# Thirteen dense products of a two-layer kernel computed by quarters, seven products instead of eight

## The chip, the core and the metric

The kernel runs on one core of a Trainium2 chip. The time is the device time of one execution, in microseconds (us). Three runs of the kernel before gave 1155.68, 1157.85 and 1160.24 us, so its median is 1157.85 us.

TensorE (PE) multiplies into PSUM, VectorE (DVE) and ScalarE (ACT) do elementwise work, GpSimd (POOL) does elementwise work that reads and writes only SBUF, and SyncE (SP) issues the large transfers.

## What is computed

256 tokens of width 1024 in float32 pass through two blocks. Cut to what matters here:

```python
# block 1
proj = rms_norm(x, norm_w) @ w_in
u_s, z_s, q, k, v, z_a, r_s, r_a = split(proj)
y_s = (s5_branch(u_s, ...) * silu(z_s)) @ w_ssm_out        # units so0, so1
y_a = (dilated_attention(q, k, v) * silu(z_a)) @ w_attn_out  # unit ao
m = sigmoid(r_s) * y_s + sigmoid(r_a) * y_a
x = x + m @ w_o                                             # units wo0, wo1
# block 2
proj = rms_norm(x, norm_mix) @ w_in_2    # ..., gate_hg: ghg0, ghg1; gate_da: gda0, gda1
y_hg = (rms_norm(hgrn2(...)) * silu(hog)) @ w_branch_hg     # unit bhg
y_da = rms_norm(diff_attention(...)) @ w_branch_da          # unit bda
mixed = sigmoid(gate_hg) * y_hg + sigmoid(gate_da) * y_da
x = x + mixed @ w_out                                       # units wout0, wout1
x = x + hier_moe(rms_norm(x, norm_moe), router, w1, w3, w2) # 32 experts, 4 at a time
```

## The kernel before

**Units.** Every dense weight is cut on the host into units of 128 x 4096 numbers (2 MB), in the list `FRONT` (line 197). A unit is either 1024 rows by 512 columns (eight blocks of 128 rows), or, for `ao`, `bhg` and `bda`, 512 rows by 1024 columns (four blocks). The units pass through three slots of a ring in SBUF, one after the other. SP loads unit n into slot n % 3 when TensorE has finished unit n - 3 (`load_unit`, line 288); SP's queue keeps the order in which it is written.

**A dense unit on TensorE** is `project` (line 301): for each half of the tokens (128 of 256) and each 512 columns, eight (or four) matmuls of 128 x 128 by 128 x 512 add up in one PSUM bank. Two banks, 0 and 1, take turns (`pj`), two more (`tp`) take transposes. A unit is 16 such matmuls; float32 makes the profile show each matmul as two records, so a unit is 32 records. VectorE or ScalarE reads the bank when it is full and frees it.

**Order of the work.** There is no scheduler: each engine's program is written out by hand and the engines meet at semaphores. After the state-space part and the attention of block 1, TensorE does glu0, glu1, za, then so0, so1, ao; VectorE multiplies each result by its gate (lines 1159, 1167, 1170) into `m_tok`; TensorE transposes it (line 894), ScalarE copies it out as `mT` (line 701), and TensorE does wo0 and wo1, whose results VectorE adds to `xres` (line 1184). Block 2 starts with hf, hq, dq, dk, hi, dv, hog, with the norm and rotation of dq and dk on VectorE (`norm_rope2`, line 1649) between them: TensorE transposes dk only when VectorE has rotated it (`dqk_ready`). Then come eight pieces of differential attention (`da_pieces`), and with each piece one half of a gate unit (ghg0, ghg1, gda0, gda1) so that TensorE has work while VectorE and ScalarE do the softmax. Then bhg, bda (VectorE lines 1765, 1773, 1776), four transposes, wout0, wout1 (line 1781), the router's logits, the choice of experts.

**The experts.** 96 units of 2 MB follow. Ten of them (`AHEAD`) are loaded before the first is used: into the slots of the ring that are free and two other places. SP issues the first of these behind the last load of a dense unit (wout1, which waits for bhg), so none of them starts before about 647 us. From the second use on, a slot is filled again as soon as TensorE has used it (line 342).

**GpSimd** scales and rotates in block 1 (lines 532 to 548) and later only issues small transfers.

## Time and profile before

| | |
|---|---|
| median of three runs | 1157.85 us |
| the profiled execution, its own time | 1155.91 us |
| its span | 1154.0 us |
| TensorE busy | 978.7 us (85%) |
| VectorE busy | 447.0 us (39%) |
| ScalarE busy | 252.0 us (22%) |
| GpSimd busy | 164.8 us (14%) |
| DMA, from 740 us on | about 428 GB/s in nearly every slice |
| granted TensorE clock, mean | 0.941 |

The profile shows one execution. Its span runs from the first to the last instruction, and the execution's own time is 1.9 us longer. Until about 700 us TensorE works nearly without pause and the transfers are light; from about 715 us on the transfers never pause and TensorE works in bursts.

### The profile page before, as it was taken

How to read it: one execution, taken by the hardware profiler on the slowest of the kernel's cores; microseconds unless marked ns; L12 is line 12 of the kernel's file. 1: busy time of each engine (PE TensorE's matmuls, PEld its weight loads, DVE VectorE, ACT ScalarE, POOL GpSimd, SP SyncE). 2: the span in 40 equal slices, each digit the busy share in tenths (PEclk: the TensorE clock that was granted, in tenths of full speed). 3: DMA queues.
4: the chain of work that ended last, by engine and by line, in shares of the span. 5: the costliest groups of instructions: out<-in, count | busy, mean ns of one | idle time of the engine just before them, and what ended most of it. 6: DMA issues, size and time to landing. Idle time of an engine off the chain costs nothing. (4 is left out here: it accounts for less than half of the span.)

```text
span 1154.0 us, 11360 instructions
## 1 busy us (share of the span) xinstructions
PE 978.7 (85%) x4440; PEld 478.6 (41%) x4440; DVE 447.0 (39%) x743; ACT 252.0 (22%) x613; POOL 164.8 (14%) x123
## 2 busy tenths in 40 slices
PE   8999999999989999999899999867585757575755
PEld 7644444446878446644444446312121212121211
DVE  6869999986622123353622413201010101010201
ACT  4464757333421012232122011000000000000000
POOL 1856666661000010000000000000000000000000
PEclk9999999999999999999999998988888988888788
DMA  9333242334224433443132695999999999999996
GB/s 365 154 145 146 74 146 80 139 146 121 74 93 164 166 105 135 154 156 144 57 146 92 272 400 199 430 426 428 430 427 428 427 428 428 430 428 429 428 428 282
DMA packets 22316, 292.84 MB, mean 254 GB/s; under 512 B 2752, under 2 KB 2816, under 8 KB 4480
## 3 DMA queue, kind: packets, MB, share of 16 engines
q1 hardware_dynamic: 21728, 291.69, 62.2%
q0 software_dynamic: 544, 0.56, 0.6%
q8 instruction: 29, 0.48, 0.2%
q14 instruction: 15, 0.12, 0.0%
HBM read 291.18 MB, written 1.05 MB: 253 GB/s over the span
## 5 line engine op out<-in xcount | busy, mean ns | idle before, releaser
L1967 PE MATMUL psum<-mem 128*32 128x512 f32 x1016 | 145.7, 706 | 84.1 <-DMA mem<-in_experts 84.0
L305 PE MATMUL psum<-mem,hT 128*128 128x512 f32 x416 | 183.9, 598 | 1.6 <-ACT xres L645 1.6
L312 PE MATMUL psum<-mem,hT 128*128 128x512 f32 x288 | 126.7, 596 | 2.8 <-ACT xn L645 1.6
L305 PE MATMUL psum<-mem 128*128 128x512 f32 x288 | 125.2, 593 | 2.4 <-ACT mem L1381 1.5
L305 PEld LDWEIGHTS psum<-mem,hT 128*128 128x128 f32 x416 | 78.4, 192 | 95.9 <-issue 95.8
L1986 PE MATMUL psum<-mem 128*32 128x512 f32 x512 | 79.6, 753 | 35.7 <-DMA mem<-in_experts 31.6
L1967 PEld LDWEIGHTS psum<-mem 128*32 128x32 f32 x1016 | 31.1, 119 | 180.3 <-DMA mem<-in_experts 118.5
L312 PEld LDWEIGHTS psum<-mem,hT 128*128 128x128 f32 x288 | 55.7, 196 | 68.3 <-issue 68.3
L305 PEld LDWEIGHTS psum<-mem 128*128 128x128 f32 x288 | 54.2, 190 | 69.0 <-issue 65.1
L319 PE MATMUL psum<-hT,mem 128*128 128x256 f32 x256 | 57.6, 382 | 0.0
L2088 DVE TENSOR_TENSOR mem<-mem,psum 128x512 f32<-128x512 f32 x8 | 5.5, 688 | 129.6 <-PE psum L1967 129.6
L1037 DVE TENSOR_TENSOR_SCAN mem<-small,mem 128x256 f32<-128x256 f32 x64 | 54.3, 909 | 0.0
L1986 PEld LDWEIGHTS psum<-mem 128*32 128x32 f32 x512 | 15.7, 125 | 90.0 <-DMA mem<-in_experts 51.4
L319 PEld LDWEIGHTS psum<-hT,mem 128*128 128x128 f32 x256 | 48.0, 190 | 7.0
L2094 DVE TENSOR_TENSOR xres<-xres,psum 128x512 f32<-128x512 f32 x32 | 22.0, 688 | 72.1 <-PE psum L1998 72.1
L2085 DVE SCALAR_TENSOR_TENSOR mem<-mem,psum 128x512 f32<-128x512 f32 x8 | 5.5, 688 | 89.5 <-ACT mem L1899 89.5
L1998 PE MATMUL psum<-mem 128*128 128x512 f32 x64 | 34.1, 657 | 6.2 <-ACT mem L1903 6.2
L1901 ACT ACTIVATE mem<-psum 128x512 f32<-128x512 f32 x8 | 4.8, 597 | 147.8 <-PE psum L1977 147.8
L1954 PE MATMUL psum<-mem,xn 128*128 128x128 f32 x256 | 30.6, 278 | 7.3 <-DVE xres L2094 6.8
L1897 ACT ACTIVATE mem<-psum 128x256 f32<-128x256 f32 x8 | 3.1, 384 | 146.1 <-PE psum L1973 146.1
L1954 PEld LDWEIGHTS psum<-mem,xn 128*128 128x128 f32 x256 | 29.2, 192 | 13.2 <-issue 11.6
L1903 ACT ACTIVATE mem<-psum 128x512 f32<-128x512 f32 x8 | 4.8, 597 | 128.0 <-PE psum L1986 128.0
(372 smaller groups left out, 1194.0 us busy)
## 6 DMA issues: line engine op xcount, KB each, us to landing
mem<-in_experts SPq DMA_DIRECT2D x95, 2048.0 KB, 35.5
mem<-in_front SPq DMA_DIRECT2D x39, 2048.0 KB, 7.7
mem<-in_front SPq DMA_DIRECT2D x2, 1024.0 KB, 9.9
xn<-in_xT SPq DMA_DIRECT2D x1, 1024.0 KB, 6.3
mem<-in_ssm_b SPq DMA_DIRECT2D x2, 512.0 KB, 11.9
mem<-in_ssm_c SPq DMA_DIRECT2D x2, 512.0 KB, 17.8
xres<-in_x SPq DMA_DIRECT2D x1, 1024.0 KB, 9.6
mem<-in_experts SPq DMA_DIRECT2D x1, 1024.0 KB, 22.2
```

The source lines that it names most:

```text
L305: ins = pe.matmul(dst, lhs[:, k, P * i:P * i + P], w[:, k, c0:c0 + 512], start=(k == 0), stop=(k == nk - 1))
L312: ins = pe.matmul(dst, tokens[:, k, i], w[:, k, :], start=(k == 0), stop=(k == KD - 1))
L319: ins = pe.matmul(dst, w[:, k, P * m:P * m + P], rhs[:, k, :], start=(k == 0), stop=(k == nk - 1))
L1037: ins = dve.tensor_tensor_scan(out=dst[:, b, c], data0=m, data1=src[:, c], initial=0.0, op0=ALU.mult, op1=ALU.add)
L1901: act.activation(hidT_, banks[7], ACT.Copy, scale=0.5).then_inc(hidT_ready, 1)
L1954: ins = pe.matmul(banks[4 + k // 4][:, P * (k % 4):P * (k % 4) + P], xn[:, i, P * k:P * k + P], sel_[:, P * i:P * i + P], start=(i == 0), ...
L1967: ins = pe.matmul(banks[m // 4][32 * q:32 * q + 32, :], xgT[:, k, 32 * q:32 * q + 32], w[q][:, FF * kk:FF * kk + FF], start=(k == 0), stop ...
L1986: ins = pe.matmul(banks[2 + c][32 * q:32 * q + 32, :], hidT[:, k, 32 * q:32 * q + 32], w[q][:, 512 * kk:512 * kk + 512], start=(k == 0), s ...
L1998: pe.matmul(banks[6 + n % 2], selT_[:, P * (n % 2):P * (n % 2) + P], y_[:, 512 * (n // 2):512 * (n // 2) + 512], start=True, stop=True).th ...
L2085: dve.scalar_tensor_tensor(out=act_, in0=th_, scalar=1.0, in1=banks[0], op0=ALU.add, op1=ALU.mult).then_inc(act_ready, 1)
L2088: dve.tensor_tensor(hid_, act_, banks[1], ALU.mult).then_inc(hid_ready, 1)
L2094: dve.tensor_tensor(dst, dst, banks[6 + n % 2], ALU.add).then_inc(added, 1)
```

## The change

Thirteen units (`QUARTERED`: so0, so1, ao, wo0, wo1, ghg0, ghg1, gda0, gda1, bhg, bda, wout0, wout1) are no longer computed by `project`. Activation and weights are split into quarters: tokens in two halves, rows of the weight in two halves, columns in two halves. Seven products of quarters replace eight (Strassen's scheme in Winograd's form):

- s1 = x21 + x22, s2 = s1 - x11, s3 = x11 - x21, s4 = x12 - s2 of the activation, once for each activation, on VectorE (`sums_of`);
- t1 = w12 - w11, t2 = w22 - t1, t3 = w22 - w12, t4 = w21 - t2 of every unit's weights, on GpSimd (`sum_weights`), with 128 x 1024 numbers each;
- P1 = x11 w11, P2 = x12 w21, P3 = s4 w22, P4 = x22 t4, P5 = s1 t1, P6 = s2 t2, P7 = s3 t3 on TensorE (`products`);
- the four quarters of the result from P1 + P2, P1 + P6 + P3 + P5, P1 + P6 + P7 + P5, P1 + P6 + P7 + P4 on VectorE. ScalarE copies P1 and P5 out of PSUM first.

A product of a unit of eight blocks is four matmuls of 128 x 128 by 128 x 256, one of a unit of four blocks is two matmuls by 128 x 512. The products go in the order 1, 5, 6, 2, 3, 7, 4 through three PSUM banks in turn, so the fourth product waits until the first has been taken, and so on across units (`after_taken`); wo0 and wout0 begin with product 4.

The weight sums take 3 x 1024 columns of SBUF, for block 2 those of ring slot 3, so the expert units of slots 3 and 4 are loaded later (slot 3 after wout1, slot 4 after `m2_done`). In the attention pieces the order of VectorE's and TensorE's work changes: the scores use one pair of banks instead of two.

```diff
         def load_unit(sp, n):
             s = n % SLOTS_BLOCKS
             if n >= SLOTS_BLOCKS:
-                pj.to_read(sp, last_fill[FRONT[n - SLOTS_BLOCKS][0]])
+                after_unit(sp, FRONT[n - SLOTS_BLOCKS][0])
...
+        def sums_of(dve, X, x):
+            x11, x12, x21, x22 = halves_of(X)
+            s1, s2, s3, s4 = x_sums[x]
+            link(dve, dve.tensor_tensor(s1, x21, x22, ALU.add), sums_ready)
+            link(dve, dve.tensor_tensor(s2, s1, x11, ALU.subtract), sums_ready)
+            mark(dve.tensor_tensor(s4, x12, s2, ALU.subtract), sums_ready)
+            link(dve, dve.tensor_tensor(s3, x11, x21, ALU.subtract), sums_ready)
+
+        def sum_weights(pool, n):
...
+            pool.wait_ge(slot_loaded[order[name] % SLOTS_BLOCKS], 16 * (order[name] // SLOTS_BLOCKS + 1))
+            if j >= 2:
+                pool.wait_ge(product_full, full(n - 2, 4))
+            pool.tensor_tensor(t1, w12, w11, ALU.subtract).then_inc(weights_ready, 1)
+            pool.wait_ge(weights_ready, sums_done(n, 1))
+            if j >= 1:
+                pool.wait_ge(product_full, full(n - 1, 6))
+            pool.tensor_tensor(t2, w22, t1, ALU.subtract).then_inc(weights_ready, 1)
+            pool.wait_ge(weights_ready, sums_done(n, 2))
+            if j >= 1:
+                pool.wait_ge(product_full, full(n - 1, 5))
+            pool.tensor_tensor(t4, w21, t2, ALU.subtract).then_inc(weights_ready, 1)
+            pool.tensor_tensor(t3, w22, w12, ALU.subtract).then_inc(weights_ready, 1)
+
+        def multiply(pe, n, p, lhs, rhs):
+            nk = lhs.shape[1]
+            for k in range(nk):
+                ins = pe.matmul(product_bank(n, p), lhs[:, k, :], rhs[:, k, :], start=(k == 0), stop=(k == nk - 1))
+            ins.then_inc(product_full, 1)
...
+        def take_p6(dve, n):
...
+            dve.tensor_tensor(p16, p1, product_bank(n, 6), ALU.add).then_inc(taken, 1)
+        def put_11(dve, n, dst):
...
+            dve.tensor_tensor(dst, taken_of(n)[0], product_bank(n, 2), ALU.add).then_inc(taken, 1)
+        def put_12(dve, n, dst):
...
+            dve.tensor_tensor(dst, taken_of(n)[2], product_bank(n, 3), ALU.add).then_inc(taken, 1)
+        def add_p5(dve, n, dst):
...
+            return dve.tensor_tensor(dst, dst, taken_of(n)[1], ALU.add)
+        def take_p7(dve, n):
...
+            dve.tensor_tensor(p167, p16, product_bank(n, 7), ALU.add).then_inc(taken, 1)
+        def sum_22(dve, n, dst):
...
+            return dve.tensor_tensor(dst, taken_of(n)[1], taken_of(n)[3], ALU.add)
+        def put_21(dve, n, dst):
...
+            dve.tensor_tensor(dst, taken_of(n)[3], product_bank(n, 4), ALU.add).then_inc(taken, 1)
...
+        def use_quarters(dve, n, use, then=None):
+            take_p6(dve, n)
+            use_11(dve, n, use, then)
+            use_12(dve, n, use, then)
+            take_p7(dve, n)
+            use_22(dve, n, use, then)
+            use_21(dve, n, use, then)
...
             pe.wait_ge(glu_used, 8)
-            project_all(["so0", "so1"], PJ_SO, gs)
+            for j in range(2, 4):
+                pj.after_read(pe, PJ_ZA + j)
+            ORDER, TURNED = ORDERS["so0"], ORDERS["wo0"]
+            for n in range(2):
+                products(pe, n, gs, X_GS, ORDER)
             pe.wait_ge(oa_ready, 4)
...
+            products(pe, nth["ao"], oaT, X_OA, ORDER)
...
@@ the second block, SyncE
-            sp.wait_ge(m_done, 4)
-            load_ahead(sp, 3)
...
+            tp.to_read(sp, TP_HG + 1)
+            load_ahead(sp, 6)
+            load_ahead(sp, 7)
+            da.to_read(sp, 7)
+            load_ahead(sp, 5)
...
+            load_ahead(sp, 3)
@@ the second block, VectorE
             norm_rope2(1)
+            dve.wait_ge(hT2_ready, 1)
+            sums_of(dve, hT, X_H2)
```

In `use_11` and its three neighbours VectorE then multiplies the finished quarter by its gate; for wo0, wo1, wout0 and wout1 (`add_to_x`) it adds the parts to `xres`, eleven operations a unit.

GpSimd, behind the last of its scaling work of block 1. Before, its program goes from seven small transfers to five more and ends:

```order
L554 DMA small<-in_da_out_norm 128x128
L554 DMA small<-in_da_lambda 128x256
L1336 DMA small<-in_norm_moe 128x8x1 [waits lam_in]
L1336 DMA small<-in_w_router_group 128x8x4
L1336 DMA small<-in_w_router_expert 128x8x32
```

Now the sums of five units stand between them (L543 is t1, L547 t2, L551 t4, L552 t3); of these, so0, so1 and the start of ao:

```order
L838 DMA small<-in_da_lambda 128x256
L543 TENSOR_TENSOR mem<-mem 128x1024 [waits slot2_loaded,s_full]
L547 TENSOR_TENSOR mem<-mem 128x1024 [waits weights_ready]
L551 TENSOR_TENSOR mem<-mem 128x1024 [waits weights_ready]
L552 TENSOR_TENSOR mem<-mem 128x4x256
L543 TENSOR_TENSOR mem<-mem 128x1024 [waits slot0_loaded]
L547 TENSOR_TENSOR mem<-mem 128x1024 [waits product_full,weights_ready]
L551 TENSOR_TENSOR mem<-mem 128x1024 [waits product_full,weights_ready]
L552 TENSOR_TENSOR mem<-mem 128x4x256
L543 TENSOR_TENSOR mem<-mem 128x1024 [waits product_full,slot1_loaded]
```

Four operations of 128 x 1024 a unit are added, 52 in all, all with both inputs and the output in SBUF.

VectorE, the results of so0, so1 and the start of ao. Before (`th_s` is the gate, pj0 and pj1 the two banks):

```order
L1159 SCALAR_TENSOR_TENSOR mem<-mem,psum 128x512 [waits th_s_ready,pj0_full]
L1159 SCALAR_TENSOR_TENSOR mem<-mem,psum 128x512 [waits th_s_ready,pj1_full]
L1159 SCALAR_TENSOR_TENSOR mem<-mem,psum 128x512 [waits th_s_ready,pj0_full]
L1159 SCALAR_TENSOR_TENSOR mem<-mem,psum 128x512 [waits th_s_ready,pj1_full]
L1167 SCALAR_TENSOR_TENSOR mem<-mem,psum 128x512 [waits pj0_free,th_a_ready,pj0_full]
```

Now, so0 alone (L615 takes P6, L621 P7, L626 adds P2, L632 P3, L647 P4; L637 and L642 add P5; L1442 is the gate):

```order
L615 TENSOR_TENSOR mem<-mem,psum 128x256 [waits p1_copied,product_full,th_s_ready,sums_ready]
L626 TENSOR_TENSOR mem<-mem,psum 128x256 [waits taken,product_full]
L1442 SCALAR_TENSOR_TENSOR mem<-mem 128x256 [waits taken]
L632 TENSOR_TENSOR mem<-mem,psum 128x256 [waits taken,product_full,q_step]
L637 TENSOR_TENSOR mem<-mem 128x256 [waits taken,p5_copied]
L1442 SCALAR_TENSOR_TENSOR mem<-mem 128x256 [waits q_step]
L621 TENSOR_TENSOR mem<-mem,psum 128x256 [waits taken,product_full,q_step]
L642 TENSOR_TENSOR mem<-mem 128x256 [waits taken,p5_copied]
L1442 SCALAR_TENSOR_TENSOR mem<-mem 128x256 [waits q_step]
L647 TENSOR_TENSOR mem<-mem,psum 128x256 [waits taken,product_full]
L1442 SCALAR_TENSOR_TENSOR mem<-mem 128x256 [waits taken]
```

Two operations of 128 x 512 a unit, each with one input in PSUM, have become eleven of 128 x 256: five with an input in PSUM and six with both inputs in SBUF.

TensorE, the end of so0 and the start of so1. Before (the second half of the tokens of so0, then so1):

```order
L305 MATMUL psum<-mem 128x512 [waits pj1_free]
L305 MATMUL psum<-mem 128x512 x7
L305 MATMUL psum<-mem 128x512 [waits pj0_free,slot0_loaded]
L305 MATMUL psum<-mem 128x512 x7
L305 MATMUL psum<-mem 128x512 [waits pj1_free]
```

Now (P3, P7 and P4 of so0, then P1, P5 and P6 of so1):

```order
L557 MATMUL psum<-mem 128x256 [waits sums_ready,p5_copied]
L557 MATMUL psum<-mem 128x256 x3
L557 MATMUL psum<-mem 128x256 [waits sums_ready,weights_ready,taken]
L557 MATMUL psum<-mem 128x256 x3
L557 MATMUL psum<-mem 128x256 [waits weights_ready,taken]
L557 MATMUL psum<-mem 128x256 x3
L557 MATMUL psum<-mem 128x256 [waits taken,slot0_loaded]
L557 MATMUL psum<-mem 128x256 x3
L557 MATMUL psum<-mem 128x256 [waits sums_ready,weights_ready,taken]
L557 MATMUL psum<-mem 128x256 x3
L557 MATMUL psum<-mem 128x256 [waits sums_ready,weights_ready,taken]
L557 MATMUL psum<-mem 128x256 x3
```

Sixteen matmuls of 512 columns a unit have become 28 of 256, and every group of four waits for VectorE (`taken`) or ScalarE (`p1_copied`, `p5_copied`) to have taken the group three before it.

## Rows read from the trace of the kernel before

**Rows 1.** The page: busy time by engine, and GB/s in 40 slices.
```profile
PE 978.7 (85%) x4440; PEld 478.6 (41%) x4440; DVE 447.0 (39%) x743; ACT 252.0 (22%) x613; POOL 164.8 (14%) x123
...
GB/s 365 154 145 146 74 146 80 139 146 121 74 93 164 166 105 135 154 156 144 57 146 92 272 400 199 430 426 428 430 427 428 427 428 428 430 428 429 428 428 282
```

**Rows 2.** TensorE in order, 325 to 420 us: start, length, line, records, wait.
```profile
356.70 13.98 PE L319 MATMUL psum<-hT,mem 128*128 128x256 f32 x64
370.52 41.36 PE L305 MATMUL psum<-mem 128*128 128x512 f32 x96
413.39 1.09 PE L894 MATMUL psum<-con,mem 128*128 128x128 f32 x8 [1.51 <-DVE mem L1170]
```

**Rows 3.** TensorE in order of time, 408 to 575 us.
```profile
416.67 20.84 PE L305 MATMUL psum<-mem 128*128 128x512 f32 x48 [0.73 <-ACT mem L701]
...
438.22 7.03 PE L305 MATMUL psum<-mem 128*128 128x512 f32 x16
...
530.63 1.04 PE L1444 MATMUL psum<-con,mem 128*128 128x128 f32 x8
...
559.48 7.13 PE L305 MATMUL psum<-mem,hT 128*128 128x512 f32 x16
570.28 0.33 PE L1541 MATMUL psum<-con,mem 128*128 128x128 f32 x1 [3.66 <-DVE mem L1736]
```

**Rows 4.** TensorE in order of time, 560 to 715 us.
```profile
582.78 7.03 PE L305 MATMUL psum<-mem,hT 128*128 128x512 f32 x16
...
599.53 7.03 PE L305 MATMUL psum<-mem,hT 128*128 128x512 f32 x16
...
633.04 7.03 PE L305 MATMUL psum<-mem 128*128 128x512 f32 x16
...
649.01 13.97 PE L305 MATMUL psum<-mem 128*128 128x512 f32 x32 [0.78 <-ACT mem L1381]
...
667.72 20.84 PE L305 MATMUL psum<-mem 128*128 128x512 f32 x48 [0.74 <-ACT mem L1381]
```

**Rows 5.** The chain that ended last, from 700 us: start, length, what.
```profile
714.66 7.07 PE psum L1967 x64
...
736.68 29.91 DMA mem<-in_experts
```

**Rows 6.** Vector engine by shape, 320 to 715 us: busy, mean ns, wait.
```profile
L1146 DVE TENSOR_TENSOR mem<-mem 128x256 f32<-128x256 f32 x8 | 3.4, 425 | 0.3
...
L1776 DVE TENSOR_TENSOR mem<-mem 128x512 f32<-128x512 f32 x4 | 2.8, 692 | 0.1
...
L1705 DVE TENSOR_TENSOR mem<-mem,small 128x1024 f32<-128x1024 f32 x2 | 2.4, 1224 | 0.1
```

**Rows 7.** GpSimd by shape, the whole span.
```profile
L533 POOL TENSOR_TENSOR mem<-mem 128x1024 f32<-128x1024 f32 x2 | 4.4, 2217 | 0.0
```

**Rows 8.** GpSimd in order of time, 159 to 176 us.
```profile
162.40 1.26 POOL L547 TENSOR_TENSOR mem<-mem 128x512 f32<-128x512 f32 x1
163.74 1.59 POOL L548 TENSOR_TENSOR mem<-mem 128x512 f32<-128x512 f32 x1
```

**Rows 9.** Vector engine in order of time, 159 to 176 us.
```profile
161.22 0.69 DVE L1026 TENSOR_TENSOR mem<-mem,psum 128x512 f32<-128x512 f32 x1
...
162.54 1.67 DVE L1028 TENSOR_TENSOR mem<-mem 128x512 f32<-128x512 f32 x1
```

**Rows 10.** Vector engine in order of time, 500 to 575 us.
```profile
523.75 0.42 DVE L1662 TENSOR_TENSOR xn<-mem,con 128x256 f32<-128x256 f32 x1
...
528.81 0.42 DVE L1667 TENSOR_TENSOR mem<-xn 128x256 f32<-128x256 f32 x1
539.27 0.69 DVE L1679 SCALAR_TENSOR_TENSOR mem<-mem,psum 128x512 f32<-128x512 f32 x1 [10.04 <-ACT mem L1393]
```

**Rows 11.** SyncE, 515 to 540 us: start of the first, length, count.
```profile
516.21 14.94 SPq L293 DMA_DIRECT2D mem<-in_front  x2
```

**Rows 12.** Transfers of line 293, 480 to 600 us: issue to landing.
```profile
DMA to landing us min/median/max: 7.4/7.7/8.1
```

More of the change, by code:

```diff
@@ L427, in build @@
                         + [(f"glu{n}", PJ_GLU + 4 * n + 3) for n in range(2)]
-                        + [(f"so{n}", PJ_SO + 2 * n + 1) for n in range(2)]
-                        + [("za", PJ_ZA + 3)]
-                        + [("ao", PJ_AO + 3)] + [(f"wo{n}", PJ_WO + 2 * n + 1) for n in range(2)]):
+                        + [("za", PJ_ZA + 3)]):
             last_fill[name] = s
+        QUARTERED = ("so0", "so1", "ao", "wo0", "wo1", "ghg0", "ghg1", "gda0", "gda1", "bhg", "bda", "wout0", "wout1")
@@ new lines, in build, with product_bank @@
+        FIRST_BANK = {"so0": 0, "so1": 7, "ao": 0, "wo0": 14, "wo1": 20, "ghg0": 0, "ghg1": 7, "gda0": 14, "gda1": 21,
+                      "bhg": 0, "bda": 7, "wout0": 0, "wout1": 0}
+        def product_bank(n, p):
+            name = QUARTERED[n]
+            width = 2048 // blocks_of(n)
+            if ORDERS[name][0] == p == 4:
+                return banks[0][:, 0:width]
+            at = ORDERS[name].index(p) - (1 if ORDERS[name][0] == 4 else 0)
+            three = (0, 1, 6) if name in GATES else (4, 5, 6) if name in ("ao", "bhg", "bda") else (6, 7, 5) if name == "wout1" else (1, 2, 3)
+            return banks[three[(FIRST_BANK[name] + at) % 3]][:, 0:width]
@@ new lines, in taken_of @@
+        def taken_of(n):
+            name, width = QUARTERED[n], 2048 // blocks_of(n)
+            part = lambda ap: [whole[:, 0:width] for whole in four(ap)]
+            if n < OF_FIRST:
+                return part(area[:, 16896:18944]) + [area[:, 13824:14336] if name == "ao" else area[:, 18688:18944]]
+            if name in GATES:
+                return part(xn[:, 1, :]) + [None]
+            return part(work[:, 2048:4096] if n < nth["wout0"] else area[:, 12288:13312]) + [xn[:, 1, 0:512]]
@@ new lines, in use_12, with use_22 @@
+        def use_12(dve, n, use, then=None):
+            c12 = taken_of(n)[4]
+            put_12(dve, n, c12)
+            link(dve, add_p5(dve, n, c12), q_step)
+            link(dve, use(0, 1, c12), q_step)
+            if then:
+                then(0, 1)
+        def use_22(dve, n, use, then=None):
+            p5 = taken_of(n)[1]
+            link(dve, sum_22(dve, n, p5), q_step)
+            use(1, 1, p5).then_inc(taken, 1)
+            dve.wait_ge(taken, used(n, C22))
+            if then:
+                then(1, 1)
@@ L1590, in _ @@
-            pe.wait_ge(m2_done, 4)
-            turn(TP_M2, 4, by_k(m2))
-            for s in range(2):
-                tp.after_read(pe, TP_M2 + 2 + s)
+            products(pe, nth["bda"], daT, X_DA, ORDER)
+            turn_quarters(pe, TP_M2, m2, m2_done)
+            for s in range(TP_M2, TP_M2 + 2):
+                tp.after_read(pe, s)
+            n0, n1 = nth["wout0"], nth["wout1"]
+            products(pe, n0, m2T, X_M2, TURNED[0:1])
+            for s in range(TP_M2 + 2, TP_M2 + 4):
+                tp.after_read(pe, s)
@@ new lines, in _, with of_hg @@
+                if a == 3:
+                    for s in range(2):
+                        tp.after_read(dve, TP_HG + s)
+                    sums_of(dve, hgT, X_HG)
+            put_21(dve, nth["gda1"], gate(3)[:, 1, 0:256])
+            da_out(*pieces[7][0:3])
+            da.after_read(dve, 7)
+            norm_sums(oda_, ods_ready)
+            def of_hg(i, half, src):
+                c = slice(512 * half, 512 * half + 512)
+                return dve.scalar_tensor_tensor(out=m2[:, i, c], in0=th_hg[:, i, c], scalar=1.0, in1=src, op0=ALU.add, op1=ALU.mult)
@@ new lines, in of_da, with both @@
+            def of_da(i, half, src):
+                c = slice(512 * half, 512 * half + 512)
+                return dve.scalar_tensor_tensor(out=th_da[:, i, c], in0=th_da[:, i, c], scalar=1.0, in1=src, op0=ALU.add, op1=ALU.mult)
+            def both(i, half):
+                c = slice(512 * half, 512 * half + 512)
+                dve.tensor_tensor(m2[:, i, c], m2[:, i, c], th_da[:, i, c], ALU.add).then_inc(m2_done, 1)
+            n = nth["bhg"]
+            take_p6(dve, n)
+            norm_out(oda_, odr_ready, ogain).then_inc(oda_ready, 1)
@@ new lines, in _ @@
+            dve.wait_ge(gates_ready, 2)
+            use_11(dve, n, of_hg)
+            use_12(dve, n, of_hg)
+            take_p7(dve, n)
+            use_22(dve, n, of_hg)
+            for s in range(2):
+                tp.after_read(dve, TP_DO + s)
+            sums_of(dve, daT, X_DA)
+            use_21(dve, n, of_hg)
+            dve.wait_ge(gates_ready, 4)
+            use_quarters(dve, nth["bda"], of_da, both)
+            for s in range(TP_M2, TP_M2 + 4):
+                tp.after_read(dve, s)
```

497 lines of the change are left out of this document (334 added, 163 removed).

## The prediction

> **What bounds the kernel now.** I read the page first. TensorE is busy 978.7 of 1154 us, and from the slice at 721 us on the transfers run at 428 GB/s without a gap [rows 1]. So there are two stages with different limits. The chain that ended last shows the border: the first use of an expert unit stands at 714.66 us, and from 736.68 us on the chain is made of transfers [rows 5]. After the first two units are used, 86 units are still to come, each 2.10 MB at 428 GB/s = 4.9 us, 421 us in all. Nothing in the change touches them. They start when TensorE frees the first slots, so **the end moves by as much as the first use of an expert unit moves**, if the ten units loaded ahead are there by then. They are: six now go out behind each other from the end of bhg on and are done about 20 us later, slot 4 follows `m2_done`, and behind wout1 come the slots 1 or 2 and 3 and half a unit, 2.5 x 4.9 = 12 us, while TensorE needs the first expert unit 18 us after wout1 (667.72 + 28.4 = 696.1 us to 714.66 us).
>
> Before the border TensorE is the limit [rows 2 to 4], with short waits for VectorE and ScalarE where one unit feeds the next (1.51 us at 413.39 us, 3.66 us at 570.28 us). VectorE and GpSimd are half idle there. The question is therefore what thirteen units cost TensorE, and what now waits for VectorE.
>
> **What TensorE saves.** A record of 512 columns costs 41.36 / 96 = 0.431 us, one of 256 columns 13.98 / 64 = 0.218 us [rows 2], weight load hidden in both. A unit was 32 x 0.431 = 13.8 us. It becomes 56 x 0.217 = 12.1 us (or 28 x 0.431 = 12.1), so 1.7 us less, 13 times: 22 us. A product of quarters is 1.73 us.
>
> **What VectorE and GpSimd get.** VectorE without a neighbour needs 0.42 us for 128x256, 0.69 for 128x512, 1.22 for 128x1024 with both inputs in SBUF [rows 6], and 0.69 for 128x512 with one in PSUM [rows 9]. Eleven operations a unit are 4.7 us, or 7.6 us for a unit of four blocks, below the 12.1 us of TensorE. GpSimd's four sums cost four times 2.2 us [rows 7] = 8.8 us, also below. If they ran side by side, little would be lost.
>
> They don't run side by side. At 162.54 us VectorE issues an addition with both inputs in SBUF. GpSimd has been at work on an SBUF operation since 162.40 and ends at 163.66; the addition ends at 164.21, 1.67 us instead of 0.69: it has waited for the whole of GpSimd's operation. GpSimd's next one, due at 163.74, takes 1.59 instead of 1.26 [rows 8, 9]. The addition at 161.22, with one input in PSUM, takes its 0.69 us beside a busy GpSimd [rows 9]. So additions with both inputs in SBUF and GpSimd's sums take turns, and a queued sum gets in between two such additions that wait for one another by a semaphore. GpSimd's operations were 1.3 us there; the new sums are 2.2 us.
>
> The Trainium skill, page "SBUF — State Buffer", section "Who interferes with whom", gives the rule: a VectorE instruction with two SBUF inputs and a GpSimd instruction that reads SBUF exclude each other for the whole instruction, one with a single SBUF input does not take part. By it the gate multiplications from SBUF (SCALAR_TENSOR_TENSOR) are blocked too, which no row here shows; with them free the sum below would be about 12 us less.
>
> Of VectorE's eleven operations a unit, six have both inputs in SBUF. When are GpSimd's sums due? t2 waits for P6 of the unit before, t4 and t3 follow at once, t1 of the next unit waits for P4. So in each unit they run from its 5.5th us to past its end, exactly when VectorE takes the results. I work each stretch out from its start, in us, with 0.3 us from the last matmul to VectorE's start.
>
> *so0, so1, ao* (before 370.52 to 416.67, 46.2 us). First a new wait: banks 1 to 3 are shared with za, whose last result goes through ScalarE and VectorE, 1.2 us. Then, with so0 at 0: t2(so1) 5.5 to 7.7; first gate operation to 8.1; t4 to 10.3; add P5 to 10.7; t3 to 12.9; gate to 13.4; take P7 to 13.9; t1(ao), due at 12.4, to 15.6; sum_22 16.0, gate 16.5, P4 taken 17.0. so1 has begun at 12.1, its P6 needs the bank of so0's P4 and is due at 15.6: it waits to 17.1. So so1 ends at 25.7 instead of 24.2, ao likewise at 39.2. Behind ao the same chain is 15 operations of 0.72 us (with the sums of the two branches) and four sums: from P6 at 32.6, the last addition ends at 50.1. Transposes of one half, then wo0 at 50.8. With 1.2 in front: 52.0, **+5.8**. Without taking turns it would end at 43.3, -2.9.
>
> *wo0, wo1* (416.67 to 445.1, 28.4). Two units and a transpose 25.2; only wo1's t2, t4, t3 stand against `add_to_x`; wo1's first two products wait 2.3 us. **-0.9**; without turns -3.4.
>
> *dk.* GpSimd may start on ghg0's four sums when ghg0 lands: issued at 516.21 [rows 11], 7.7 us on its way [rows 12], 524 us. There VectorE rotates dk, from 523.75 twelve linked operations of 128x256, both inputs in SBUF, until 529.2 [rows 10], and TensorE transposes it at 530.63, 1.4 us later [rows 3]. Four sums of 2.1 to 2.2 us get in between: 8.4 us, so dk is ready at 537.6 and TensorE waits **7.0**. Nothing later is idle to take it back. This one hits nothing that the change speaks of, it is only in the way.
>
> `sums_of(hT)` (four of 0.69) stands in VectorE's gap of 10 us before 539.27 us [rows 10] and costs nothing; if dk comes late it still has 14 us of hog beside it.
>
> *Gates* (559.48 to 633.04, 73.6 us: 23.3, then three pairs of 16.75 [rows 3, 4]). The first combine now goes before the norm, so the 3.66 us wait goes. But the mask of piece 1 comes behind three operations of 1.22 us and t2, t4 of ghg1, at 14.5 us, and since one pair of banks serves the scores, TensorE's scores(2) wait for it from 9.9 us; exponent, combine and P2 follow: the pair takes 23.2 us. Each later pair is 12.1 + 2.5 for scores, values, transposes = 14.6, plus 2.4 because P4 waits for P2 to be taken behind a combine with three SBUF operations that wait for t2 and t3: 17.0. Sum 74.2, **+0.6**; without turns 18.8 + 3 x 14.6 = 62.6, -11.0.
>
> *bhg, bda* (633.04 to 667.72, 34.7). bhg with its transposes 15.7. bda's P5 needs the bank of P7 and s1 of daT, which VectorE reaches behind norm (two of 1.22 between t2, t4, t3), four gate operations and t1(wout0): 22.3 instead of 18.1. bda ends at 33.1, and as behind ao the last addition is 10.5 us later; wout0 at 44.3. **+9.6**; without turns -0.9.
>
> *wout0, wout1* as wo0, wo1: **-0.9**; without turns -3.4.
>
> Sum with strict turns: 5.8 - 0.9 + 7.0 + 0.6 + 9.6 - 0.9 = +21.2 us. I take 2 us off, because unlinked additions can pass in one gap of GpSimd: +19. The profiled execution was 1155.9 us (span 1154.0, and 1.9 around it), 1.9 below the median of 1157.85: 1155.9 + 19 = **1175 us**.
>
> **Rivals.**
> - *The sums are cheap.* VectorE and GpSimd hardly meet, because VectorE's queue runs ahead or the scaling's pattern (broadcast inputs) was what made GpSimd hold it. Then -2.9 - 3.4 + 0 - 11.0 - 0.9 - 3.4 = -21.6, 1134 us. For it: VectorE's idle share of 61% [rows 1]. Against it: rows 8 and 9, and the semaphore behind nearly each addition.
> - *Half of it.* Turns are taken, but the gate multiplications go free, or stalls in one unit push the sums of the next out of the way. Then dk and the norms still pay, the tails pay half: about 0, 1148 to 1164 us, here 1156.
> - *GpSimd becomes the bound.* Its 1024-wide operation takes 2.6 us instead of 2.2 (half in the way, strided quarters); about 22 of its 52 sums stand on the chain, 22 x 0.4 = 9 us more, and four a unit with VectorE's turns come to 13 us, above the 12.1 of TensorE: it decides from there on. 1155.9 + 21 + 9 = 1186 and up to 1195 us. The slower side in the extreme.
> - *The 256-column matmuls don't cost half,* the weight load shows. [Rows 2] speak against it, 0.218 to 0.431; I give it nothing of its own.
>
> **Chances.** Forecast 0.52 (1164 to 1188), cheap sums 0.20 (1130 to 1148), half 0.18, GpSimd the bound 0.10. The range: 1143 to 1190 leaves most of the cheap case below and half of the last above. A measurement tells 0.5%, 5.8 us, from no change. Faster than 1152: 0.20 + a third of the half case = 0.26. Within: 0.11. Slower than 1163.6: 0.52 + 0.10 and the rest, 0.63.
>
> **What would show it.** In the trace after: dense units of 56 records at 0.218 us. VectorE's two-SBUF-input additions of 128x256 with a mean of 1 us or more, those from PSUM at 0.42 to 0.48. TensorE idle about 7 us before the transpose of dk, 10 us before wo0 and before wout0, 1.5 us inside so1 and ao. First use of an expert unit at about 733 us, and from there the same 430 us to the end. Wrong would be: two-input additions at 0.42 us (then cheap sums), or a first expert use that moves without the end moving.

## The result and the profile after

The changed kernel takes 1190.72 us (median of 4 runs, 1187.65 to 1199.75) against 1157.08 us of the kernel before in the same session (1155.68 to 1160.24). The ratio is 1.0285, with a 95% interval of 1.0242 to 1.0328: **slower by 2.9%, some 33 us**. Forecast were 1175 us and a range up to 1190: the right side, some 16 us too little of it, and just outside the range.

The profiled execution took 1187.65 us (span 1185.9), the lowest of its four times. The page of the changed kernel (compare [rows 1]; PEclk is the granted TensorE clock in tenths, slice by slice):

```profile
PE 972.4 (82%) x4668; PEld 528.5 (45%) x4668; DVE 580.1 (49%) x874; ACT 262.9 (22%) x635; POOL 294.8 (25%) x175
...
PEclk9999999999999979998999878998888888878788
...
GB/s 368 145 133 142 81 133 141 93 158 87 117 91 150 175 107 124 161 142 71 72 142 83 273 248 217 375 429 426 429 426 429 427 429 429 429 427 429 428 429 286
```

TensorE should have lost 22 us of busy time and lost 6. VectorE is busy 133 us longer and GpSimd 130. VectorE has 131 operations more; the kernel without the weight sums (below) has the same 874 and is busy 504.6 us with them, 58 us longer than before. The other 75 of the 133 us is time in which an operation counts as running and waits. The stream of the experts' weights at 428 GB/s begins one slice later than before.

TensorE in order of time (start, length, line, records, the wait before them), to be read against [rows 2 to 4]:

```profile
416.00 1.09 PE L1581 MATMUL psum<-con,mem 128*128 128x128 f32 x4 [5.43 <-DVE mem L1453]
418.76 1.11 PE L1581 MATMUL psum<-con,mem 128*128 128x128 f32 x4 [1.67 <-DVE mem L1453]
...
422.47 13.38 PE L557 MATMUL psum<-mem 128*128 128x256 f32 x56
...
438.90 8.58 PE L557 MATMUL psum<-mem 128*128 128x256 f32 x32 [3.05 <-DVE xres L692]
...
545.41 1.97 PE L1759 MATMUL psum<-con,mem 128*128 128x128 f32 x8 [6.59 <-DVE mem L1986]
547.17 15.83 PE L311 MATMUL psum<-mem,hT 128*128 128x512 f32 x32
...
577.12 1.97 PE L557 MATMUL psum<-mem,hT 128*128 128x256 f32 x8 [0.41 <-issue]
...
631.02 1.99 PE L557 MATMUL psum<-mem,hT 128*128 128x256 f32 x8 [2.28 <-DVE mem L626]
...
672.25 13.06 PE L557 MATMUL psum<-mem 128*128 128x512 f32 x24 [3.90 <-DVE mem L530]
690.74 1.09 PE L1581 MATMUL psum<-con,mem 128*128 128x128 f32 x4 [5.43 <-DVE mem L2110]
...
714.46 3.35 PE L557 MATMUL psum<-mem 128*128 128x256 f32 x8 [3.05 <-DVE xres L692]
...
746.71 0.62 PE L2318 MATMUL psum<-hT,mem 128*32 128x512 f32 x2
```

Every new wait of more than 1.6 us has VectorE as its releaser: behind ao (5.43 and 1.67), within the wo pair (3.05), before the dk transposes (6.59), in the later pairs of gates (2.28 to 2.88), in bhg (1.77), in bda (3.90), behind bda (5.43 and 1.67), within the wout pair (3.05). None has GpSimd. The last row is the first use of an expert: 746.71 us in place of 714.66 [rows 5], so **32.05 us later**. From there to the end of the span it is 439.2 us, before 439.3. The border between the stages held.

What VectorE and GpSimd did before the dk transposes, in the changed kernel, GpSimd first:

```profile
531.98 2.43 POOL L543 TENSOR_TENSOR mem<-mem 128x1024 f32<-128x1024 f32 x1 [90.13 <-DMA mem<-in_front]
534.49 2.40 POOL L547 TENSOR_TENSOR mem<-mem 128x1024 f32<-128x1024 f32 x1
536.98 2.41 POOL L551 TENSOR_TENSOR mem<-mem 128x1024 f32<-128x1024 f32 x1
539.34 2.52 POOL L552 TENSOR_TENSOR mem<-mem 128x1024 f32<-128x1024 f32 x1
```

```profile
531.77 0.43 DVE L1981 TENSOR_TENSOR xn<-mem,con 128x256 f32<-128x256 f32 x1
532.23 2.46 DVE L1982 TENSOR_TENSOR xn<-mem,con 128x256 f32<-128x256 f32 x1
534.72 2.45 DVE L1983 TENSOR_TENSOR xn<-mem,con 128x256 f32<-128x256 f32 x1
537.21 2.45 DVE L1984 TENSOR_TENSOR xn<-mem,con 128x256 f32<-128x256 f32 x1
539.70 2.44 DVE L1985 TENSOR_TENSOR mem<-xn 128x256 f32<-128x256 f32 x1
542.18 0.42 DVE L1986 TENSOR_TENSOR mem<-xn 128x256 f32<-128x256 f32 x1
```

Four operations of VectorE take 2.45 us, the ones before and behind them 0.42 to 0.43. Each ends some 0.3 us behind the end of a GpSimd sum. Four sums, four operations held up, one each: turns. Both engines show as busy all the while.

### The profile page after: what moved, and what is told of

Read it like the earlier page. It is cut to its first block and busy times, and to the rows that moved or that the text cites. A ratio compares the mean times of both kernels' runs of the same rounds, so it can differ in the third digit from the quotient of the medians.

```text
span 1185.9 us, 12251 instructions
## 1 busy us (share of the span) xinstructions
PE 972.4 (82%) x4668; PEld 528.5 (45%) x4668; DVE 580.1 (49%) x874; ACT 262.9 (22%) x635; POOL 294.8 (25%) x175
## 5 line engine op out<-in xcount | busy, mean ns | idle before, releaser
L557 PE MATMUL psum<-mem 128*128 128x256 f32 (+1 forms) x452 | 128.8, 442 | 15.2 <-DVE xres L692 6.1
L311 PE MATMUL psum<-mem,hT 128*128 128x512 f32 x288 | 128.0, 602 | 1.6 <-ACT xres L931 1.6
L318 PE MATMUL psum<-mem,hT 128*128 128x512 f32 x288 | 126.7, 596 | 2.9 <-ACT xn L931 1.6
L557 PEld LDWEIGHTS psum<-mem 128*128 128x128 f32 x452 | 89.3, 202 | 48.5 <-issue 29.5
L318 PEld LDWEIGHTS psum<-mem,hT 128*128 128x128 f32 x288 | 55.7, 196 | 68.3 <-issue 68.3
L311 PEld LDWEIGHTS psum<-mem,hT 128*128 128x128 f32 x288 | 54.8, 193 | 69.2 <-issue 69.0
L543 POOL TENSOR_TENSOR mem<-mem 128x1024 f32<-128x1024 f32 x13 | 32.2, 2476 | 196.6 <-DMA mem<-in_front 180.7
L547 POOL TENSOR_TENSOR mem<-mem 128x1024 f32<-128x1024 f32 x13 | 31.5, 2424 | 114.7 <-PE psum L557 114.5
L2441 DVE COPY mem<-psum 128x512 f32<-128x512 f32 x8 | 5.5, 691 | 70.6 <-PE psum L2337 70.6
L827 POOL TENSOR_TENSOR mem<-mem 128x512 f32<-128x512 f32 x16 | 21.7, 1354 | 72.5 <-DVE mem L1317 52.2
L2349 PE MATMUL psum<-mem 128*128 128x512 f32 x64 | 33.4, 645 | 6.2 <-ACT mem L2254 6.2
L2252 ACT ACTIVATE mem<-psum 128x512 f32<-128x512 f32 x8 | 4.8, 597 | 148.0 <-PE psum L2328 148.0
```

The costliest lines, as they stand in the source:

```text
L311: ins = pe.matmul(dst, lhs[:, k, P * i:P * i + P], w[:, k, c0:c0 + 512], start=(k == 0), stop=(k == nk - 1))
L318: ins = pe.matmul(dst, tokens[:, k, i], w[:, k, :], start=(k == 0), stop=(k == KD - 1))
L543: pool.tensor_tensor(t1, w12, w11, ALU.subtract).then_inc(weights_ready, 1)
L547: pool.tensor_tensor(t2, w22, t1, ALU.subtract).then_inc(weights_ready, 1)
L557: ins = pe.matmul(product_bank(n, p), lhs[:, k, :], rhs[:, k, :], start=(k == 0), stop=(k == nk - 1))
L827: link(pool, pool.tensor_tensor(Hr[:, b], cos_t[:, b], scan_re[:, b], ALU.mult), pool1)
```

## The experiments

My theory at this point was that of the prediction: an operation of VectorE with both inputs in SBUF and a GpSimd sum exclude each other and take turns, and VectorE's chains, late for that, stop TensorE. New was a second part: the granted clock. From 650 to 697 us, core 0, the changed kernel and then the kernel before (PE, PEld, DVE, ACT, POOL busy, then PEclk, DMA share, GB/s):

```profile
650.00:697.00 47.00, 32.68 (x87) 15.62 (x86) 36.83 (x37) 7.41 (x13) 24.21 (x9) 0.83 0.68 273
```

```profile
650.00:697.00 47.00, 44.51 (x128) 21.07 (x126) 8.25 (x12) 5.54 (x13) 0.00 (x0) 1.00 0.87 372
```

Before, the clock stood at 1.00, all of it at 2.4 GHz; now it is 0.83, part of the stretch at 1.2 GHz. The rival theories were that VectorE's added operations alone are too many, that GpSimd's sums come late by themselves, or that TensorE is slow behind the waits for another reason than its clock.

Three of the kernels below (without the sums, with copies, with memsets) leave the weight sums out and compute other numbers; they serve for their times alone.

**Without the sums.** The body of `sum_weights` is left out, and TensorE multiplies plain quarters:

```
-            t1, t2, t3, t4 = weight_sums_of(n)
+            t1, t2, t3, t4 = w12, w22, w12, w21
-                    pe.wait_ge(weights_ready, sums_done(n, ...))
```

> Left out: the 52 weight sums on GpSimd; TensorE multiplies plain quarters in their place, so the numbers differ and the count of instructions on TensorE and VectorE does not. Theory (the loss is made by VectorE taking turns with GpSimd's sums, and the rest of it by the clock that falls after the waits so made): first use of an expert, 746.7 us in the changed kernel, falls to 680 to 690, since the units then cost what my no-turns terms say (-2.9, -3.4, 0, -11.0, -0.9, -3.4, sum -21.6 from 714.7, so 693; less what the clock no longer loses), and the whole run is 1130 to 1140 us, faster than before. Rival A (VectorE's own added operations, not the turns, make the loss): first use of an expert stays above 725 and the run above 1168. Rival B (GpSimd's sums are late by themselves and TensorE waits for them, not for VectorE): also near 1135, but VectorE's operations on two SBUF inputs would keep their length in the tail of ao (2.71 us each); the theory wants them at 1.2.

Measured: 1131.76 us, ratio to before 0.9773 (0.9739 to 0.9808). The first expert is used at 690.48 us. My sum without turns was 1134. VectorE's operations behind ao were back at the lengths of before (my text said 1.2 us for these 512 columns; alone they take 0.69):

```profile
404.35 0.69 DVE L1429 SCALAR_TENSOR_TENSOR mem<-mem 128x512 f32<-128x512 f32 x1
405.08 0.69 DVE L1433 SCALAR_TENSOR_TENSOR mem<-mem 128x512 f32<-128x512 f32 x1
```

So the seven products and VectorE's work are worth 26 us, and the 52 sums cost 59. The rival of VectorE's added operations falls: they are all still here. The rival of the late sums had these operations stay at 2.71 us, and in the trace of the changed kernel no wait of TensorE between ao and the first expert has GpSimd as its releaser.

**What of a GpSimd operation holds VectorE up.** All four subtractions are replaced by a copy of one quarter, or by a memset, of the same shape:

```
-            pool.tensor_tensor(t1, w12, w11, ALU.subtract).then_inc(weights_ready, 1)
+            pool.tensor_copy(t1, w12).then_inc(weights_ready, 1)      # one kernel
+            pool.memset(t1, 0.0).then_inc(weights_ready, 1)           # the other
```

> GpSimd copies one quarter where it subtracted two (one input from SBUF in place of two), so the numbers differ. Theory (two reading inputs are needed on GpSimd's side too): as without the sums, VectorE's operations at 1.2 us, first use of an expert at 685 to 695. Rival (one input is enough): VectorE's operations in the tail of ao wait for the copy's length, 1.2 us plus what the copy takes, and first use of an expert stays above 700.

> GpSimd writes zeros where the weight sums stood (a memset of the same shape, nothing read), so the numbers differ. Asks what of GpSimd's work makes VectorE take turns. Theory (it is reading two operands from SBUF): VectorE's two-input operations in the tail of ao take 1.2 us again in place of 2.71, first use of an expert at 685 to 695. Rival (any GpSimd operation holds the SBUF port): they still wait for the memset's length, and first use of an expert lies above 700.

Measured: copy 1137.35 us (0.9818), first expert at 696.62; memset 1129.57 us (0.9750), first expert at 688.45. With the copies, GpSimd and then VectorE:

```profile
405.49 1.04 POOL L552 COPY mem<-mem 128x1024 f32<-128x1024 f32 x1
```

```profile
405.75 1.32 DVE L1449 SCALAR_TENSOR_TENSOR mem<-mem 128x512 f32<-128x512 f32 x1
407.11 0.69 DVE L1453 SCALAR_TENSOR_TENSOR mem<-mem 128x512 f32<-128x512 f32 x1
```

With the memsets:

```profile
406.94 0.95 POOL L543 MEMSET mem<- 128x1024 f32 x1 [4.01 <-PE psum L557]
```

```profile
407.39 0.69 DVE L642 TENSOR_TENSOR mem<-mem 128x512 f32<-128x512 f32 x1
```

The multiplication that came 0.26 us behind a copy's start took 1.32 us: it waited until about the copy's end. The addition inside a memset's time took its 0.69. So one operand read from SBUF is enough, and writing alone does nothing. VectorE's busy time over the whole run says the same of all the operations: 580.1 us in the changed kernel, 520.1 with copies, 504.8 with memsets, 504.6 without sums. For the copy this is the rival's mechanism; its bound of 700 us was mine and wrong, because a copy takes 1.04 us where a sum takes 2.35, and VectorE waited 15.5 us for copies in all and 75.5 for sums. The Trainium skill, "SBUF — State Buffer", section "Who interferes with whom", says the same: a VectorE instruction with two SBUF inputs contends with a GpSimd instruction that reads SBUF, and not with one that only writes it. By that rule the gate multiplications take part too, and the trace agrees: L1453 took 2.71 us in the changed kernel and 0.69 without the sums. That page of the Trainium skill frees a VectorE instruction with a single SBUF input only outside the 2-port perf modes, a condition that the prediction left out and that no run here tests.

**The first gate unit's sums by themselves.** First, one line in the changed kernel, ahead of the sums of the second block:

```
             pool.wait_ge(m_done, 4)
+            pool.wait_ge(dqk_ready.sem, 2)
             for n in range(OF_FIRST, len(QUARTERED)):
```

> One line more: GpSimd begins the four weight sums of the first gate unit only once the operands of the dk transposes are there. Theory: TensorE's 6.59 us wait before the dk transposes goes, and with it the 2.8 us that the following 36 records took longer at the lower clock: 9.6 us together, 1181 us (ratio to before 1.0205). The sums then run beside dk's 64 products of TensorE, 16.7 us, and are done before the first gate product. Rival A (the wait only moves: the first gate unit then waits for its sums): 0 to 3 us, 1188 to 1190, with a wait of 5 us or more before the first product with a weight sum. Rival B (clock does not answer to the wait): 6.6 us, 1184, with the 32 records after it still at 15.8 us.

Measured: 1180.91 us, 9.8 less than the changed kernel's 1190.72, ratio to before 1.0190 (1.0155 to 1.0225). The wait before the dk transposes is gone, the records behind it take 13.90 us, and there is no wait before the first gate product:

```profile
542.25 1.04 PE L1760 MATMUL psum<-con,mem 128*128 128x128 f32 x8
543.12 13.90 PE L311 MATMUL psum<-mem,hT 128*128 128x512 f32 x32
```

Then the reverse: the kernel before, with these four sums alone (two waits of SyncE for them, before transfers into the places that they use, are left out here):

```
+            pool.wait_ge(slot_loaded[n % SLOTS_BLOCKS], 16 * (n // SLOTS_BLOCKS + 1))
+            for c, (x, y) in enumerate(((w12, w11), (w22, t[0]), (w21, t[1]), (w22, w12))):
+                pool.tensor_tensor(t[c], x, y, ALU.subtract).then_inc(spare_sums, 1)
```

> The kernel before, with only the four GpSimd sums of the first gate unit's weights added (results unused), in the place where the changed kernel has them. Theory: they alone make the wait before the dk transposes, 6.6 us, and 2.8 us through the clock behind it: 9 to 10 us over the kernel before, 1167 us. Rival A (the wait needs the whole change, for instance the later landing of transfers or VectorE's backlog): under 2 us, 1157 to 1159. Rival B (the turns cost but TensorE keeps its clock): 6.6 us, 1164.

Measured: 1166.41 us, ratio 1.0077 (1.0049 to 1.0106), 8.7 us; in its trace the first expert is used at 724.51 us, 9.85 later.

```profile
537.56 1.97 PE L1457 MATMUL psum<-con,mem 128*128 128x128 f32 x8 [6.68 <-DVE mem L1680]
539.32 15.88 PE L306 MATMUL psum<-mem,hT 128*128 128x512 f32 x32
```

Taken out or put in, four sums that no product needs for over 30 us make the same wait and the same slow 40 records. The two waits of SyncE cost nothing: from the first matmul of bhg to the first expert it is 81.65 us, in the kernel before 81.62. The kernel that has them alone is measurably slower than the kernel before.

**The clock's own part.** The waits stay, but TensorE works through them, on an unused bank: first at dk alone, then also in the two waits behind ao and behind bda and in those within the wo and the wout pair.

```
             project_all(["dv"], PJ_DV, hT)
+            for _ in range(14):
+                pe.matmul(banks[7][:, 0:256], ident, con[:, 0:256], start=True, stop=True)
             pe.wait_ge(dqk_ready.sem, 2)
```

> Fourteen matmuls of 256 columns into an unused bank ahead of the wait before the dk transposes, about 6 us of TensorE, so that it works where it waited 6.59 us. The wait for VectorE itself stays. Theory (the clock falls after the wait): the 32 records behind take 13.9 us again in place of 15.8 and the transposes 1.0 in place of 2.0; time 1188 us, 2.8 less. Rival (the records behind are slow for another cause, GpSimd's sums or the DMA in SBUF): no change in them, 1190.5.

> The changed kernel with matmuls into an unused bank wherever TensorE waited over 3 us on the path: 11 and 3 ahead of the two waits in each tail (ao, bda), 6 ahead of wo1 and of wout1, 14 ahead of the dk transposes. The waits for VectorE stay. Measures what the clock alone took. Theory (a lower clock behind each wait is a cost of its own): dk 2.9 us as with its matmuls alone, the wo pair 1.2 + 1.5, the wout pair 2.0 + 1.5 + 0.3: 9 us, 1181 to 1183. Rival (only the wait before dk mattered, the others are slow for the port or the transfers): 1187 to 1188.

Measured: 1187.76 us (ratio 1.0251, 1.0216 to 1.0285) and 1181.89 us (1.0206, 1.0172 to 1.0240). The first of these intervals overlaps that of the changed kernel, so its 3.0 us rest on the rows:

```profile
542.13 6.21 PE L1803 MATMUL psum<-con 128*128 128x256 f32 x28
548.91 1.09 PE L1759 MATMUL psum<-con,mem 128*128 128x128 f32 x8 [0.57 <-DVE mem L1988]
549.84 13.90 PE L311 MATMUL psum<-mem,hT 128*128 128x512 f32 x32
```

VectorE is as late as ever, but the transposes take 1.09 us in place of 1.97 and the 32 records 13.90 in place of 15.83. With all these places filled, the stretch from the transposes behind ao (415.88 us there) to the first expert (738.91) is 323.0 us, in the changed kernel 330.7 (416.00 to 746.71): the filling gave back 7.7 us. It is not all that the clock took, because the wait of 3.90 us in bda stayed empty. The 24 records behind that one took 13.06 us in the changed kernel at a mean granted clock of 0.80, and 10.73 at 1.00 in the kernel without sums.

**Smaller sums.** If the turns go one for one, the size of GpSimd's operation is what VectorE pays at each. So every sum was made in 2 and in 4 operations on parts of its columns:

```
+            def in_pieces(dst, a, b):
+                cols = dst.shape[2] // 2                                    # 4, 8
+                for c in range(2):
+                    part = slice(cols * c, cols * c + cols)
+                    ins = pool.tensor_tensor(dst[:, :, part], a[:, :, part], b[:, :, part], ALU.subtract)
+                ins.then_inc(weights_ready, 1)
-            pool.tensor_tensor(t1, w12, w11, ALU.subtract).then_inc(weights_ready, 1)
+            in_pieces(t1, w12, w11)
```

> Each of the 52 weight sums on GpSimd is made in two operations of half the columns. If GpSimd's 2.45 us for 1024 columns has a small fixed part, a half takes 1.25 to 1.3 us. Theory (one operation of VectorE, one of GpSimd, in turn): the wait of each VectorE operation for its turn halves, so dk's wait of 6.59 us stays near 6.6 (the same GpSimd time, 9.8 us, is alternated with more VectorE operations, each of which lets one half through), while the chains in the tails, where VectorE's operations are fewer than GpSimd's, lose 1.2 us each less: three in the tail of ao, three unlinked additions twice, some five in the tails of bhg and bda: 10 to 14 us, 1177 to 1181. Rival A (VectorE is locked out as long as GpSimd has work, whatever its pieces): no change, 1190. Rival B (the overhead of 52 more operations and the later sums decide): above 1193, with waits of TensorE for GpSimd.

> As before, in four operations of a quarter of the columns each, 0.65 us by the same rule. Theory: the waits of the tails go down again by half of what they were, 3 to 5 us less than with halves (1173 to 1178), until GpSimd, which now lets a VectorE operation in every 0.65 us, delivers its sums late to TensorE. Rival A: 1190. Rival B: above 1193 and above the time with halves.

Measured: halves 1169.25 us (1.0098, 1.0070 to 1.0125), quarters 1154.85 us (0.9966, 0.9949 to 0.9983). That is 21 and 36 us less than the changed kernel, about twice what I had expected. VectorE behind ao, in the changed kernel, with halves, and with quarters:

```profile
406.91 2.71 DVE L1453 SCALAR_TENSOR_TENSOR mem<-mem 128x512 f32<-128x512 f32 x1
...
412.42 2.71 DVE L1449 SCALAR_TENSOR_TENSOR mem<-mem 128x512 f32<-128x512 f32 x1
```

```profile
411.13 1.63 DVE L1460 SCALAR_TENSOR_TENSOR mem<-mem 128x512 f32<-128x512 f32 x1
```

```profile
409.38 1.10 DVE L1460 SCALAR_TENSOR_TENSOR mem<-mem 128x512 f32<-128x512 f32 x1
```

Less the 0.69 of the operation itself: 2.02, 0.94, 0.41 us of waiting, half of it at each halving. "Locked out as long as GpSimd has work" is refuted. The wait before the dk transposes follows the same count: 6.07 us with halves, whose eight pieces all find a turn among the chain's twelve operations, and 3.00 with quarters, whose sixteen don't. I had the tails in mind and left the gates out. From the first matmul of the gates to the first of bhg it was 73.0 us in the changed kernel, 69.9 with halves and 62.7 with quarters, so with quarters the gates gained 10 of the 36 us.

**Together.** Quarters and eighths, both with the line that delays the first gate unit's sums:

> Weight sums in quarters, and the sums of the first gate unit begun only behind the operands of the dk transposes. With quarters alone that wait was 3.0 us, with 14.81 and 1.90 us in place of 13.9 and 1.04 behind it. Theory: 4.8 us less than with quarters alone, 1150, faster than before by 0.7%. Rival: the moved sums press on a later place and the time stays at 1155.

> The same with eighths (128 columns for each partition). A GpSimd operation took 2.8, 1.44, 0.87 us as it was halved twice while VectorE took its turns; VectorE's 512-column operations 2.71, 1.64, 1.10 against 0.69 without sums. The part of GpSimd's that holds VectorE up is 2.02, 0.95, 0.41, so an eighth should hold it for 0.2 us and VectorE's operation take 0.9. Theory: the tails get 3 us shorter again, if GpSimd keeps up: 1144 to 1148. Rival: with a turn at each of its 8 pieces and 0.69 us given away at each, a sum takes 7 us, four of them 28, and TensorE waits for sums in ao and the gates: 1155 to 1170.

Measured: quarters 1147.05 us (0.9913, 0.9885 to 0.9940), eighths 1146.09 us (0.9897, 0.9869 to 0.9925). The two are not to be told apart. The moved sums gained more than the 4.8 us that I expected over quarters alone. With eighths a new wait stands before wout0, the first with GpSimd as the releaser, and slow records behind it:

```profile
658.54 6.62 PE L564 MATMUL psum<-mem 128*128 128x256 f32 x16 [2.07 <-POOL mem L540]
```

A sum's four or eight pieces each give a turn away: the 52 sums took 131 us of GpSimd's time whole, 147 in halves, 173 in quarters, 206 in eighths. So the last kernel mixes them: quarters for wo0 and wout0, eighths for the rest, the delayed sums of the first gate unit, and 3 and 6 matmuls into an unused bank (`fill`) in the two waits behind ao and behind bda:

```
+            m = 4 if QUARTERED[n] in ("wo0", "wout0") else 8
             ...
                 for i in range(2):
+                    if half:
+                        fill(pe, (3, 6)[i])
                     pe.wait_ge(done, (2, 3) [i] if half else (3, 4)[i])
```

> A version made of what the runs show: weight sums in eighths, but in quarters for wo0 and wout0 (with eighths the first product of wout0 waited 2.07 us for its sums), the first gate unit's sums begun behind the operands of the dk transposes, and 3 and 6 matmuls into an unused bank ahead of the two waits in each tail. Theory: against eighths everywhere (1146) it regains the 2.07 us before wout0, some 3 us of clock behind it (the first 16 records took 6.62 us in place of 3.62) and 1 to 2 us behind the tail of ao: 1139 to 1142, 1.3% faster than before. Rival (what is regained there comes back as a later landing of the experts' weights or as a wait for sums in another unit): 1145 to 1147.

Measured: 1142.48 us (1141.43 to 1145.91) against 1160.84 of the kernel before in that session, ratio 0.9850 (0.9827 to 0.9872): **1.5% faster than the kernel before, 4% faster than the changed kernel**. The first expert is used at 703.05 us. What each of the changes in it gave is not measured apart. The wait for GpSimd is gone, and the 16 records take 4.76 us (3.62 at the full clock):

```profile
659.31 4.76 PE L566 MATMUL psum<-mem 128*128 128x256 f32 x16
```

Where the time lies, from the traces, in us. The borders are the first transposes behind ao, the first matmul of the first gate unit, the first transposes behind bda, the first use of an expert:

| | to ao's end | gates' start | bda's end | experts | end |
|---|---|---|---|---|---|
| before | 413.4 | 146.1 | 105.0 | 50.2 | 439.3 |
| changed | 416.0 | 161.1 | 113.6 | 56.0 | 439.2 |
| halves | 412.9 | 157.0 | 106.9 | 51.3 | 439.5 |
| quarters | 410.6 | 152.9 | 97.6 | 53.3 | 439.5 |
| mixed | 413.5 | 147.8 | 90.1 | 51.7 | 439.2 |
| no sums | 408.8 | 146.2 | 86.0 | 49.5 | 439.4 |

The last column never moves: all of it is won and lost before the experts. The gates and the branches behind them hold the most, 28 us between the changed kernel and the one without sums.

## Why the prediction was nearly right, and where it failed

The mechanism was right: turns of one operation each, gate multiplications included, idle time before the dk transposes that nothing takes back, an end that moves with the first expert. **The step that failed is the sum of the turns' price: it holds a wait of TensorE at its own length and the records behind it at full speed.** In the runs they were slower at a lower granted clock. My terms with and without turns are 42.8 us apart (+21.2 and -21.6); the first expert of the changed kernel and of the one without sums are 56.2 us apart. Apart from the gates, every stretch from wo0 on came out dearer than forecast. By stretch, forecast and measured (start of each stretch, after against before, in us):

- so0, so1, ao, up to wo0 (422.47 against 416.67): +5.8 and **+5.8**. In part luck: without the sums it was -1.7 where I had -2.9, and the turns added 7.5 where I had 8.7.
- wo0, wo1 (446.52 to 454.32 behind them): -0.9 and **+2.0**. Two things were missing: the three unlinked additions of `add_to_x` did not pass in one gap of GpSimd but took a turn each (L692 from SBUF has a mean of 932 ns over 24, from PSUM 417), so the wait was 3.05 us and not 2.3; and the records ran slow: 13.38 us for 56 in place of 56 x 0.218 = 12.2, and 8.58 for 32 in place of the 7.14 that they took with the wait filled.
- dk: +7.0 and **+9.6**. The wait was 6.59, close to the forecast; 0.93 + 1.93 us come from the clock behind it.
- gates (577.12 to 650.14): +0.6 and **-0.5**. This is luck: two errors met. Without the sums the gates took 59.6 us (forecast 62.6), and the turns added 13.4 (forecast 11.6).
- bhg, bda, up to wout0 (697.13): +9.6 and **+12.3**. The wait for `sums_of` in bda, 3.90 us, stands behind the norm, whose two operations took 1.94 and 2.24 us on average, and a sum took 3.2 to 3.3 us where it had to let such an operation of 1024 columns through.
- wout0, wout1 to the first expert: -0.9 and **+2.6**. The clock is the larger part of the difference: the first 16 records took 5.64 us in place of 3.62, and the eight behind the wait 3.35 in place of the 1.97 that they took with the wait filled.

Their sum is 32 us; mine was 21.2. TensorE's own time up to the first expert shows where the 11 us between them lie. The changed kernel, the kernel before and the one without sums (PE, PEld, DVE, ACT, POOL busy, PEclk, DMA share, GB/s):

```profile
0.00:746.71 746.71, 677.64 (x2796) 439.06 (x2796) 525.42 (x787) 246.36 (x603) 294.80 (x175) 0.97 0.40 148
```

```profile
0.00:714.66 714.66, 684.48 (x2569) 388.60 (x2569) 392.29 (x656) 235.50 (x581) 164.79 (x123) 0.99 0.42 156
```

```profile
0.00:690.48 690.48, 664.38 (x2797) 433.04 (x2797) 449.87 (x787) 246.13 (x603) 164.85 (x123) 0.99 0.43 160
```

TensorE's idle time rose from 30.2 to 69.1 us, by 38.9, where my sum has about 43 (21.2, and the 22 of work saved). So the waits were not underpriced as a whole. Its busy time fell by 6.8 where I had 22, and with the same records but without the sums it falls by 20.1. The absent term is in the records: they are 13.3 us longer in the changed kernel than in the one without sums. That the clock makes all of it is not shown, but its mean is 0.97 there against 0.99, and filling the waits gave back 7.7 us.

GpSimd's operation was mis-sized too: "2.2 us" in my sum, 2.35 alone and 2.42 to 2.58 on average in its four places. How much of the end that moved is not measured. And the step "I take 2 us off, because unlinked additions can pass in one gap of GpSimd" is refuted by L692. A slip of the sum itself: the terms of the wo and wout pairs without turns, 25.2 against 28.4, give -3.2 and not -3.4.

The rival "cheap sums" was the right price for a kernel whose sums don't collide (1134 forecast, 1131.8 measured without them), and the wrong state. It holds by stretch as well: forecast -2.9, -3.4, 0, -11.0, -0.9, -3.4, measured -1.7, -3.0, +0.3, -13.9, -2.2, -3.6. "GpSimd the bound" had the right time (1186 to 1195) for a partly wrong reason: its operation is 0.2 to 0.4 us longer, but TensorE waited for VectorE at every place; waits for GpSimd itself showed only with eighths.

## What to carry to other kernels

Ask of every GpSimd operation that reads SBUF not how long its engine is idle, but which chain of VectorE runs beside it: a chain of linked operations with both inputs in SBUF pays one GpSimd operation for each of its own, as long as GpSimd has one waiting. Where the work can't go elsewhere, cut it small (here 128x1024 to 128x256 gave back 36 us) and hold it back by a semaphore from chains on the path (9.8 us for one line), until GpSimd itself is late. And price a wait of TensorE at more than its length. Not tried: making the weight sums on the host, which would load seven quarters a unit in place of four.

## What the runs showed of the hardware

- The price of a turn goes with the size of GpSimd's operation and not with that of VectorE's: 2.02, 0.94 and 0.41 us of waiting at 1024, 512 and 256 columns for each partition, the first both for an operation of 512 columns (2.71 less 0.69) and for one of 256 (2.45 less 0.42). A memset of 0.95 us cost VectorE nothing, a copy of 1.04 us with one operand held it like a sum.
- Cutting isn't free on GpSimd: with the turns, one piece took 1.44, 0.87 and 0.53 us on average at 512, 256 and 128 columns, so the same sums took 147, 173 and 206 us.
- After 6.6 us without work, TensorE's next eight transposes took 1.97 us in place of 1.04 and the 32 records behind them 15.83 in place of 13.90: 2.9 us more. With matmuls of no use in the wait it was 1.09 and 13.90. Not everywhere did that help: with the waits behind ao filled, wo0's 56 records still took 13.78 us (13.38 without). The granted clock there was 0.89 with the waits filled and 0.92 without, so the filling did not hold it up in that place. Why is open.
